# Where VectorE's masks for the next pair of heads stand against the group norm's reciprocal

## The reference

```python
def step(s, inp):
    r_t, w_t, k_t, v_t, kk_t, b_t = inp
    s_kk = jnp.einsum('bhvk,bhk->bhv', s, -kk_t)
    s = s * w_t[:, :, None, :] + s_kk[..., None] * b_t[:, :, None, :] + v_t[..., None] * k_t[:, :, None, :]
    return s, jnp.einsum('bhvk,bhk->bhv', s, r_t)
...
mean = jnp.mean(y, axis=-1, keepdims=True)
var = jnp.mean(jnp.square(y - mean), axis=-1, keepdims=True)
y = (y - mean) * lax.rsqrt(var + GN_EPS) * ln_g + ln_b
y = y + jnp.sum(r * k * r_k, axis=-1, keepdims=True) * v
out = y.reshape(bsz, t_len, A_WIDTH) * g
```

## Time and profile before

| | us |
|---|---|
| median of three runs | 2304.16 |
| lowest and highest of them | 2302.93, 2304.97 |
| the profiled execution's own time | 2305.04 |
| span of its trace | 2303.3 |
| TensorE busy | 2158.8 (94%) |
| VectorE busy | 1142.7 (50%) |
| ScalarE busy | 663.1 (29%) |
| GpSimd busy | 36.0 (2%) |

### The profile page before, as it was taken

One profiled execution on the slowest core, in us unless ns is written; L12 is line 12 of the kernel. 1 busy time (PEld: TensorE's weight loads), 2 busy tenths in 40 slices (PEclk: granted clock), 3 DMA queues, 4 the chain that ended last, 5 costly groups with the idle time before them and its releaser, 6 DMA issues.

```text
span 2303.3 us, 29512 instructions
## 1 busy us (share of the span) xinstructions
PE 2158.8 (94%) x11960; PEld 1811.7 (79%) x11960; DVE 1142.7 (50%) x1787; ACT 663.1 (29%) x751; POOL 36.0 (2%) x72
## 2 busy tenths in 40 slices
PE   5999899999999997999979997999999999979997
PEld 4999767777766665999979996677776666669996
DVE  4443435676566523444264534266755664254443
ACT  3433322122132203443344332212212421034432
POOL 0000000000000000000000000000000000000000
PEclk9999999999999998999989999999999999989998
DMA  4444231111122233344434442211112222324442
GB/s 170 153 146 165 92 110 61 65 48 64 61 86 110 103 110 110 136 156 146 147 117 158 146 165 83 100 61 47 65 65 79 91 98 99 122 92 160 148 155 87
DMA packets 37049, 251.98 MB, mean 109 GB/s; under 512 B 4609, under 2 KB 4673, under 8 KB 8161
## 3 DMA queue, kind: packets, MB, share of 16 engines
q1 hardware_dynamic: 32112, 234.60, 28.5%
q0 software_dynamic: 4848, 16.13, 1.9%
HBM read 242.05 MB, written 8.67 MB: 109 GB/s over the span
## 4 chain that ended last, share of the span: by engine, by line
PE 83%; DVE 9%; ACT 3%; DVEq 3%; DMA 1%; issue 1%; SPq 0%; ACTq 0%
PE dps L465 40%; PE dps L402 15%; PE dps L419 12%; DVE tmp L983 2%; PE mx L556 2%; PE mx L550 2%; PE mx L558 2%; PE mx L432 1%; ACT tmp L753 1%; DMA raw<-in_wstream 1%; DVE x L986 1%; ACT L753 1%; PE mx L664 1%; PE mx L674 1%; DVEq L1379 1%
## 5 line engine op out<-in xcount | busy, mean ns | idle before, releaser
L980 DVE TENSOR_TENSOR wlo<-raw,whi 128x2048 fp32r<-128x2048 f32 x136 | 311.4, 2292 | 396.7 <-ACT whi L753 389.3
L465 PE MATMUL dps<-uh,whi 128*128 128x320 f32 x1408 | 430.0, 305 | 26.7 <-DVE ul L980 26.7
L465 PE MATMUL dps<-uh,wlo 128*128 128x320 f32 x1408 | 436.4, 310 | 0.0
L465 PE MATMUL dps<-ul,whi 128*128 128x320 f32 x1408 | 435.1, 309 | 0.0
L419 PE MATMUL dps<-u,raw 128*128 128x320 f32 x1280 | 409.1, 446 | 0.0
L753 ACT ACTIVATE whi<-raw 128x2048 fp32r<-128x2048 f32 x136 | 259.8, 1912 | 327.4 <-PE dps L465 325.0
L465 PEld LDWEIGHTS dps<-uh,whi 128*128 128x128 f32 x1408 | 266.7, 189 | 29.2 <-issue 28.6
L419 PEld LDWEIGHTS dps<-u,raw 128*128 128x128 f32 x1280 | 227.7, 194 | 70.6 <-issue 12.9
L465 PEld LDWEIGHTS dps<-uh,wlo 128*128 128x128 f32 x1408 | 266.9, 190 | 0.0
L465 PEld LDWEIGHTS dps<-ul,whi 128*128 128x128 f32 x1408 | 266.1, 189 | 0.0
L465 PE MATMUL dps<-hfh,whi 128*128 128x320 f32 x704 | 221.1, 314 | 0.0
(11 more groups left out here) (249 smaller groups left out, 2229.2 us busy)
## 6 DMA issues: line engine op xcount, KB each, us to landing
raw<-in_wstream SPq DMA_DIRECT2D x220, 1024.0 KB, 4.8
hs<-in_st_hgrn POOLq DMA_DIRECT2D x8, 512.0 KB, 3.5
out_o_hgrn<-hsn POOLq DMA_DIRECT2D x8, 512.0 KB, 2.9
sw<-in_smallw POOLq DMA_DIRECT2D x2, 1024.0 KB, 8.5
ss<-in_st_rwkv POOLq DMA_DIRECT2D x8, 256.0 KB, 3.9
out_o_rwkv<-ssn POOLq DMA_DIRECT2D x8, 256.0 KB, 2.3
x<-in_xT SPq DMA_DIRECT2D x1, 1280.0 KB, 6.1
out_yT<-x SPq DMA_DIRECT2D x1, 1280.0 KB, 4.5
```

Source lines behind the costliest of these rows:

```text
L465: m = pe.matmul(dps[:, 2 * half + c, 0:T], w[:, k, c * P:(c + 1) * P], v[:, k0 + k, :], start=first and k == 0 and i == 0, stop=last and k ...
L980: return nc.vector.tensor_tensor(out, a, b, op)
```

## The change

TensorE's program: of the five pieces after the variance's matmul, one now stands ahead of the attention of chunks 2 and 3, one ahead of that of chunk 4, and three behind it. VectorE's program: all five masks of the next pair stand ahead of the wait for `sd_ready`, so ahead of the reciprocal and of all that follows it. No operation is added or taken away.

```diff
--- before.py
+++ after.py
@@ -620,12 +620,13 @@
                     attention(l, p + 1, (0, 1))
                 pe.wait_ge(S["devsq_ready"], n + 1)
                 pe.matmul(mx[:, 3, 0:T], blk, ysq, start=True, stop=True).then_inc(S["var_done"], 1)
-                dense_part(3)
+                dense_part(1)
                 if more:
                     attention(l, p + 1, (2, 3))
-                dense_part(2)
+                dense_part(1)
                 if more:
                     attention(l, p + 1, (4,))
+                dense_part(3)
 
             def hgrn_head(l, p):
                 n = l * 4 + p
@@ -1269,21 +1270,17 @@
                 dve.wait_ge(S["mean_done"], n + 1)
                 stt(dev, mx[:, 2, 0:T], -1.0 / CH, y_, ALU.mult, ALU.add).then_inc(S["dev_ready"], 1)
                 if more:
-                    masks(l, p + 1, (0, 1))
+                    masks(l, p + 1, range(NCH))
                 dve.wait_ge(S["sd_ready"], n + 1)
                 nc.vector.reciprocal(rsd, sd)
                 fence()
                 mul(dev, dev, rsd)
                 fence()
                 ts(dev, dev, pcol("rwkv_ln_g", p), ALU.mult, pcol("rwkv_ln_b", p), ALU.add)
-                if more:
-                    masks(l, p + 1, (2,))
                 fence()
                 tt(dev, dev, tile_at(oa, p), ALU.add)
                 fence()
                 mul(tile_at(oa, p), dev, tile_at(lo, p + 8)).then_inc(S["oa_ready"], 1)
-                if more:
-                    masks(l, p + 1, (3, 4))
                 fence()
 
             def rglru(l):
```

## The result

The kernel after took 2338.56 us (median of four runs, 2336.26 to 2339.72) against 2304.43 for the kernel before in the same comparison: a ratio of 1.0148, 95% interval 1.013 to 1.0165, slower by 34.1 us. The prediction had the direction, and 2331.0 with a range that ended at 2336.

The account below looks back on a forecast made before the run. The prediction took TensorE, 83% of the last-ending chain, as the bound: 18.4 of waits plus 8.4 of clock made 26.8, added to the profiled 2305.04 for 2331.8, less 0.9 for the median, 2331.0; range 2320 to 2336.

Parts of the forecast that it names:

- VectorE's order and the wait: At six pair ends the reciprocal stands behind mask 4; TensorE's transposes wait 3.70, net 3.07 a place, 18.4 in all.
- rival 1: At the six places the wait comes but the clock holds: 2322.6; chance 0.16.
- TensorE stays last: At the next pair's level 1 matmuls, TensorE is last by 1.3, so VectorE being less late gives nothing back.
- Rival 2: First level waits for VectorE's update, not the six pieces: loss 1.93 a place, 11.6 in all, 2315.8; chance 0.04.
- The queues that the change moves past: SyncE's weight load and ScalarE's read 0.9 later, GpSimd's state load 3.1 later; all three costed at nothing.
- The clock: After the new waits the granted clock falls; 1.4 taken a place within bounds of nothing and 2.04, 8.4 for six.
- the head's 1.68: Price of a clock fall: successive HGRN2 head stretches with the same work, 33.03 with a fall against 31.35 without.
- case for a clock that holds: TensorE's wait of 1.87 until 1784.63 passed with the granted clock at 1.00 in the slice at 1785.
- the dearest head's: HGRN2 head stretch of 33.39, a fall price of 2.04, taken as upper bound a place.
- rival 4: Last three pieces cover the group norm, small waits of 0.63 a place won: 2300.4; chance 0.03, plus 0.02 for faster.

Follow-up runs that it names:

- experiment 1: Changed kernel plus six 320-column matmuls on constants, never read, in TensorE's new wait for the end of the group norm; 2322.64 us, ratio 1.0083.
- Experiment 8: Changed kernel plus two matmuls on constants (1.08 us) ahead of each layer's first attention, so all places come later; 2334.4 us, ratio 1.0135.
- experiment 3: Kernel before with VectorE's new order alone, TensorE keeping the old order; 2351.21 us, ratio 1.0203.
- experiment 4: Changed kernel with three of the six pieces behind the transposes moved between the first and second transposes; 2331.93 us, ratio 1.0122.
- experiment 6: Changed kernel plus three 320-column matmuls on constants in TensorE's new wait, half of the filling; 2322.22 us, ratio 1.0077.
- experiment 7: Kernel before plus never-read matmuls on constants in TensorE's waits around the RMS norms; 2298.92 us, ratio 0.9979.
- experiment 9: Kernel before with matmuls on constants in the norm waits and four more ahead of each layer's first HGRN2 head; 2295.93 us, ratio 0.9971.

## Why the prediction was right and where it failed

**VectorE's order and the wait: right.** The reciprocal was pushed from 425.78 to 429.39 and `oa_ready` from 430.77 to 433.76; the wait is 3.45 in the trace's count, which runs from the modelled end of the last matmul, and 3.6 in the forecast's (433.81 less 430.2), where it had 3.70. The net cost was to be 3.07 a place, 18.4; it is 2.9, 17.6, and experiment 1 has it as a whole kernel, at 2322.64 where rival 1 had 2322.6.

**TensorE stays last: right.** The inverse update starts at 440.40 at the first place, held by the slow transposes and not by VectorE's own work, and level 1 follows the six pieces at 444.66. Rival 2 did not come. The queues that the change moves past cost nothing that the waits show: TensorE waits 1.2 for weight loads in all, against 1.1 before.

**The clock: right that it falls, wrong in what that costs.** The step that failed is "I take 1.4, near the head's 1.68 ... less something for slow time that runs off inside the wait", with 2.04 as its upper bound. All six places show a fall. The four at which it comes at the wait's end or behind it cost 1.53 to 1.62, which is what the heads had told. At the two at which it comes about a microsecond before the wait's end (1.3 and 1.0) it costs 4.26 and 4.44: the clock doesn't come back after 3.4 us, it stays low for 10. I had taken a fall inside the wait for the cheap case, because part of its slow time would be idle time; it is the dear one. The sum is 15.1 in place of 8.4, and these 6.7 are most of the 7.6 between 2331.0 and 2338.56.

Why it stays low is shown in part. Experiment 8 shows that the place does not decide it. Over the changed kernel and experiments 3, 4 and 8 the moment of the fall against the end of the wait sorts all 21 falls:

| fall | places | slow stretch |
|---|---|---|
| from 0.2 before the end of the wait to 1.2 behind it | 12 | 3.4 |
| 0.8 to 1.6 before it | 5 | 10.2 |
| 1.3 before it, with pieces behind it (experiment 4) | 1 | 6.8 |
| 1.9 to 2.5 before it (experiment 3) | 3 | 6.8 |

So the cost doesn't simply grow with how early the fall comes. The third row shows, at one place, that the slow stretch ends sooner when whole pieces take the transposes' place. That it is the transposes and the 64-column matmuls that keep the clock low is my reading; no run measures it by itself.

The bound was too narrow for a reason that could be seen. It was taken from heads, where the clock falls while TensorE is in the middle of work. No row of before has a fall inside a wait with small matmuls behind it, but the same trace has falls inside waits, ahead of the sums of squares of the norms, and there the slow stretch lasts 6.8 or 10.2 us and not 3.4. At the norm ahead of the mixer in layer 1 it runs from 272.1 to 282.3, five of these ten behind the wait:

```profile
277.26 7.07 PE L432 MATMUL mx<-sq,cst 128*128 128x320 f32 x16 [6.41 <-ACT sq L753]
```

```profile
273.00:277.00 4.00, 0.00 (x0) 0.00 (x0) 3.84 (x6) 0.53 (x1) 0.00 (x0) 0.50 0.00 0
277.00:281.00 4.00, 3.74 (x7) 2.53 (x8) 3.76 (x7) 1.68 (x3) 0.00 (x0) 0.50 0.01 2
281.00:285.00 4.00, 3.33 (x10) 1.88 (x8) 0.64 (x2) 1.36 (x3) 0.00 (x0) 0.83 0.00 0
```

The prediction's case for a clock that holds was also thinner than it looks: it names the 1.87 until 1784.63, without a fall, and not the same wait in layer 1, until 646.69, which is followed by one at 647.6.

The Trainium skill, "TensorE: Matmul & The Clock Gate", section "HAM oscillation — how this bites in real kernels", has every tile of its kernel begin at the low clock behind its wait. The changed kernel's trace agrees, with a fall at six places of six; experiments 4 and 8, with waits as long, have none at three of twelve. Six falls at the head's price, 6 x 1.68 = 10.1, or at the dearest head's, 12.2, would have been too low as well.

**Not slower (rival 4): refuted as argued.** The three pieces end at 430.2, and `oa_ready` comes 3.5 later.

## What to carry to other kernels

When work is moved ahead of a long operation on an in-order engine, ask what is released behind that operation, and count the masks and their waits against the cover that the waiting engine has left; here 1.6 us of pieces stood against 5.2 us of VectorE. Price a new wait on TensorE of several microseconds with the clock, take the price from falls of the same kind in the trace, and price a fall inside the wait as dearer than one behind it. Where such a wait can't be removed, matmuls that nobody reads, put into it, held the clock there in all four kernels tried here (experiments 1, 6, 7 and 9), and in experiment 6 half of the wait was enough.

## What the runs showed of the hardware that was not expected

A fall of the clock to 1.2 GHz that begins about a microsecond before TensorE's wait ends lasted 10 us and cost 4.3 to 4.4, where one at the end of the wait lasted 3.4 and cost 1.5 to 1.6. Filling 1.6 of 3.5 idle microseconds avoided the fall as well as filling all of it, 2322.22 against 2322.64. And full clock around every norm was worth only 5.2 us in this kernel, although TensorE's busy time at low clock fell from some 68 us to some 24 with it, since the sums there wait for squares and the first weights for their load.
